# Expert weights of a top-2 mixture loaded as 256-column pairs, eight transfers an expert in place of twelve

## What is computed

```python
gate = ...                                   # (T, 16), two non-zero entries a token
y = jnp.zeros_like(t)
for e in range(16):
    h = jax.nn.silu(t @ w1[e]) * (t @ w3[e])  # w1, w3: 1024 x 512
    y = y + gate[:, e:e + 1] * (h @ w2[e])    # w2: 512 x 1024
x = layer_norm(ALPHA * x + y, ln2_g, ln2_b)
```

## Time and profile before

| | us |
|---|---|
| median of 3 runs | 1128.33 (1127.29 to 1129.90) |
| the profiled execution's own time | 1126.51 |
| its span, first to last instruction | 1125.0 |
| TensorE busy (PE) | 970.7, 86% of the span |
| weight loads into TensorE (PEld) | 832.3, 74% |
| VectorE (DVE) | 705.9, 63% |
| ScalarE (ACT) | 531.7, 47% |
| GpSimd (POOL) | 186.9, 17% |
| SP's queue: 180736 packets, 139.54 MB | 42.9% of 16 DMA engines |

### The profile page before, as it was taken

The page is one execution under the profiler, slowest core; times in us unless marked ns, Lnnn a source line. Parts: engine busy times, 40 slices in busy tenths (PEclk is TensorE's granted clock), DMA queues, the critical chain, the costliest instruction groups (busy, mean ns, idle before and its releaser), DMA issues.

```text
span 1125.0 us, 17021 instructions
## 1 busy us (share of the span) xinstructions
PE 970.7 (86%) x6074; PEld 832.3 (74%) x6074; DVE 705.9 (63%) x1061; ACT 531.7 (47%) x901; POOL 186.9 (17%) x227
## 2 busy tenths in 40 slices
PE   4998999989999999899936959999999999999200
PEld 3777998967777776788836849999999999988100
DVE  3101724555556647665568648888888888885397
ACT  4112512234655546411125647667667667664232
POOL 2000000000000000000004333222332222210474
PEclk8999999989999999999956979999999999999755
DMA  9011020001010011782119999989998999965542
GB/s 241 8 55 38 20 75 20 1 20 38 19 38 20 20 38 38 211 265 91 57 38 213 132 314 304 293 281 290 287 300 277 286 282 292 278 209 204 206 180 94
DMA packets 195058, 170.87 MB, mean 152 GB/s; under 512 B 20400, under 2 KB 172976, under 8 KB 195008
## 3 DMA queue, kind: packets, MB, share of 16 engines
q1 hardware_dynamic: 180736, 139.54, 42.9%
q0 software_dynamic: 11232, 29.47, 7.4%
q10 hardware_dynamic: 3040, 1.19, 0.5%
HBM read 151.21 MB, written 18.95 MB: 151 GB/s over the span
## 4 chain that ended last, share of the span: by engine, by line
PE 76%; DVE 9%; issue 4%; ACT 4%; DMA 3%; POOL 2%; SPq 1%; POOLq 0%; DVEq 0%; ACTq 0%
PE pz L925 15%; PE bank L632 11%; PE bank L634 11%; PE bank L633 11%; PE pz L927 6%; PE pz L784 2%; PE pz L952 2%; PE pz L950 2%; PE bank L797 2%; PE bank L811 2%; PE bank L908 2%; SPq L434 1%; POOL slot_tokens L549 1%; DMA slot_tokens<-tok,rows_u 1%; PE pz L634 1%
## 5 line engine op out<-in xcount | busy, mean ns | idle before, releaser
L925 PE MATMUL pz<-xT,eh 128*128 128x320 f32 x1024 | 266.4, 347 | 2.2 <-DVE gu L1549 1.3
L1536 DVE TENSOR_TENSOR el<-er,eh 128x1024 fp32r<-128x1024 f32 x192 | 229.7, 1220 | 35.7 <-ACT eh L1187 33.5
L927 PE MATMUL pz<-xT,el 128*128 128x160 f32 x1024 | 242.4, 237 | 0.0
L1187 ACT ACTIVATE eh<-er 128x1024 fp32r<-128x1024 f32 x192 | 196.2, 1050 | 7.5 <-DMA er<-in_w_dram 6.8
L927 PEld LDWEIGHTS pz<-xT,el 128*128 128x128 f32 x1024 | 197.1, 192 | 0.6
L925 PEld LDWEIGHTS pz<-xT,eh 128*128 128x128 f32 x1024 | 193.4, 189 | 4.6 <-DVE el L1536 1.5
L1388 DVE TENSOR_TENSOR_SCAN Qs<-Qs 128x128 f32<-128x128 f32 (+7 forms) x48 | 65.0, 1354 | 78.4 <-ACT Qs L1087 78.4
L632 PE MATMUL bank<-xT_hi,w_hi 128*128 128x512 f32 x256 | 105.1, 410 | 10.2 <-DVE w_lo L1265 10.2
L634 PE MATMUL bank<-xT_hi,w_lo 128*128 128x512 f32 x256 | 101.0, 394 | 0.0
L633 PE MATMUL bank<-xT_lo,w_hi 128*128 128x512 f32 x256 | 100.6, 393 | 0.0
L526 POOL MEMSET zidl<- 128x140 uint32 x1 | 0.2, 214 | 444.7 <-ACT aT L1098 444.7
(11 more groups left out here) (261 smaller groups left out, 1847.9 us busy)
## 6 DMA issues: line engine op xcount, KB each, us to landing
er<-in_w_dram SPq DMA_DIRECT2D x192, 512.0 KB, 6.0
w_raw<-in_w_in_dram SPq DMA_DIRECT2D x21, 512.0 KB, 3.8
y_scratch<-yA POOLq DMA_DIRECT2D x16, 512.0 KB, 4.5
x_row<-in_x_dram SPq DMA_DIRECT2D x8, 512.0 KB, 8.3
xres<-in_x_dram SPq DMA_DIRECT2D x8, 512.0 KB, 4.8
x_scratch<-x SPq DMA_DIRECT2D x8, 512.0 KB, 2.9
cx<-x_scratch SPq DMA_DIRECT2D x8, 512.0 KB, 7.7
out_dram<-cx SPq DMA_DIRECT2D x8, 512.0 KB, 2.6
```

Source lines behind the costliest of these rows:

```text
L925: pe.matmul(bank, eh[:, p, ks], xT2[:, k, :, :].rearrange("p a t -> p (a t)"), start=(k == 0), stop=False, skip_group_check=True)
L927: last = pe.matmul(bank[:, 0:TW], el[:, p, ks], xT2[:, k, 0, :], start=False, stop=(k == NK - 1), skip_group_check=True)
L1187: act.activation(eh[:, p, :], er[:, p, :], ACT.Copy).then_inc(S["eh_ok"], 1)
L1536: dve.tensor_tensor(el[:, p, :], er[:, p, :], eh[:, p, :].bitcast(F32), ALU.subtract).then_inc(S["el_ok"], 1)
```

## The change

The w1 and w3 halves of an expert are loaded two column slices at a time. Transfer q (0 to 3) brings 256 columns of w1 (even q) or w3 (odd q): pieces 0 and 2, 1 and 3, 4 and 6, 5 and 7, each 1 MB with runs of 256 floats (1 KB). Transfers 4 to 7 are the w2 pieces as before. In `er` the two slots of a pair hold 8 rows of 256 columns, so that ACT and DVE read a piece as 8 runs of 128 floats at a stride of 256 (raw_piece, as_raw); `eh` and `el` keep their layout. A pair's load waits until DVE is done with the later of the two pieces it overwrites (2, 3, 6, 7).

```diff
--- before.py
+++ after.py
@@ -324,7 +324,7 @@
-        names += [f"e_in{p}" for p in range(NPIECE)]
+        names += [f"e_in{q}" for q in range(2 * NF)]
         names += [f"{n}{i}" for n in ("cg_in",) for i in range(NT)]
         S = {n: sem(n) for n in names}
 
@@ -352,6 +352,16 @@
 
         w_k = I["w_in"][0].rearrange("(k p) n -> p k n", p=P)
 
+        def raw_piece(p):
+
+            if p >= 2 * NF:
+                return er[:, p, :]
+            c0 = (p % 4 // 2) * P
+            return er[:, 4 * (p // 4) + 2 * (p % 2):4 * (p // 4) + 2 * (p % 2) + 2, :].rearrange("p a (k f) -> p (a k) f", f=2 * P)[:, :, c0:c0 + P]
+
+        def as_raw(t, p):
+            return t if p >= 2 * NF else t.rearrange("p (k f) -> p k f", k=NK)
+
         w1v = I["w1"][0].rearrange("e (k p) f -> p e k f", p=P)
         w3v = I["w3"][0].rearrange("e (k p) f -> p e k f", p=P)
         w2v = I["w2"][0].rearrange("e (f p) d -> p e f d", p=P)
@@ -359,16 +369,17 @@
         def load_expert(sp, j, e, first=False):
 
             b = NE * j + e
-            for p in range(NPIECE):
+            for q in range(NF + NF):
                 if not first:
-                    sp.wait_ge(S["el_ok"], NPIECE * b - NPIECE + p + 1)
-                if p < 2 * NF:
-                    src = (w1v, w3v)[p % 2][:, bass.ds(e, 1), :, (p // 2) * P:(p // 2 + 1) * P]
-                    dst = er[:, p:p + 1, :].rearrange("p e (k f) -> p e k f", k=NK)
+                    last = 4 * (q // 2) + 2 + q % 2 if q < NF else NF + q
+                    sp.wait_ge(S["el_ok"], NPIECE * b - NPIECE + last + 1)
+                if q < NF:
+                    src = (w1v, w3v)[q % 2][:, bass.ds(e, 1), :, (q // 2) * 2 * P:(q // 2 + 1) * 2 * P]
+                    dst = er[:, 2 * q:2 * q + 2, :].rearrange("p a (k f) -> p (a k) f", f=2 * P).unsqueeze(1)
                 else:
-                    src = w2v[:, bass.ds(e, 1), p - 2 * NF, :]
-                    dst = er[:, p:p + 1, :]
-                sp.dma_start(dst, src).then_inc(S[f"e_in{p}"], 16)
+                    src = w2v[:, bass.ds(e, 1), q - NF, :]
+                    dst = er[:, NF + q:NF + q + 1, :]
+                sp.dma_start(dst, src).then_inc(S[f"e_in{q}"], 16)
 
         def passes_of(eng, one_pass):
 
@@ -1181,10 +1192,10 @@
 
 
             def piece_hi(b, p):
-                act.wait_ge(S[f"e_in{p}"], 16 * b + 16)
+                act.wait_ge(S[f"e_in{2 * (p // 4) + p % 2 if p < 2 * NF else p - NF}"], 16 * b + 16)
                 if not (isinstance(b, int) and b == 0):
                     act.wait_ge(S["piece_done"], NPIECE * b - NPIECE + p + 1)
-                act.activation(eh[:, p, :], er[:, p, :], ACT.Copy).then_inc(S["eh_ok"], 1)
+                act.activation(as_raw(eh[:, p, :], p), raw_piece(p), ACT.Copy).then_inc(S["eh_ok"], 1)
 
             def x_hi(b, rounds=range(NXR)):
                 for r in rounds:
@@ -1533,7 +1544,7 @@
 
             def piece_lo(b, p):
                 dve.wait_ge(S["eh_ok"], NPIECE * b + p + 1)
-                dve.tensor_tensor(el[:, p, :], er[:, p, :], eh[:, p, :].bitcast(F32), ALU.subtract).then_inc(S["el_ok"], 1)
+                dve.tensor_tensor(as_raw(el[:, p, :], p), raw_piece(p), as_raw(eh[:, p, :].bitcast(F32), p), ALU.subtract).then_inc(S["el_ok"], 1)
 
             def x_lo(b, rounds=range(NXR)):
                 for r in rounds:
```

## The result

The changed kernel takes 1130.70 us, the median of 20 runs (1127.68 to 1133.43), against 1128.23 for the kernel before (20 runs beside it, 1126.22 to 1130.60): ratio 1.0021, 95% interval 1.0013 to 1.0030. It is slower by 0.21%, some 2.4 us, just past what a measurement can tell from nothing. The forecast was 1127.4 and no change.

What follows compares the result with a forecast made beforehand. TensorE bounds the expert stage, except in one dip set by three DMA waits. Terms: 0 steady, 0 strides, 0.9 us less in the dip, giving 1125.6 for the profiled execution and 1127.4 for the median; range 1118.6 to 1133.3.

Steps and rivals of the forecast that it cites:

- The dip: TensorE's 11.96 us stop near 650 us behind scatter, list read and gather; 0.9 us less was forecast there.
- the 11.96: TensorE's stop in us for the gather of expert 2's rows, taken to cover ACT's 4.71 us wait.
- The third rival: In the dip: a pair comes too late for ACT, past some 8 us of cover; slower by 1 or 2 us; chance 0.03.
- The second rival: Scatters of the slot list: longer weight packets ahead of them, slower by 3.3 us, 1131.6; chance 0.22.
- The first rival: In the dip: all three DMA waits scale with a weight byte's time, 3.7 us faster, 1124.6; chance 0.37.
- The sum's 0 for the scatter: In the dip: weight bytes don't fill the engines, so fewer, longer packets shouldn't shorten the scatter: 0.
- 0 in the steady part: From 700 to 1000 us TensorE hides the loads, so faster transfers and later release change nothing.
- 0 for the strides: ACT's and DVE's strided reads of w1 and w3 pieces cost the same as contiguous ones, within one percent.
- 0 for expert 0's load: At 468 us, ahead of later xres loads: 2.1 us shorter, no TensorE time hangs on it, cost 0.
- 65,536 packets fewer: SP's queue in the profile after would have this many packets fewer than its 180,736.
- the estimate: Loads of w1 and w3: 1 KB packets run near 340 GB/s, 2.1 us less an expert, 14% less time a byte.
- the sum's 0.9 us less for the gather: In the dip: the gather's 6.20 us wait scales with the 14% less time a weight byte, 0.9 us less.

Runs made afterwards that it cites:

- the gather gone: Expert 2's rows fetched behind the scatters with expert 1's row numbers, without waiting for the slot list: kernel before 1118.29 us (0.9924), changed kernel 1123.36 us (0.9971).
- the late release alone: Kernel before with its twelve 512-byte-run transfers, but the pairs' release and order (0, 2, 1, 3): 1129.68 us, ratio 1.0016.
- strides: Changed layout and strided reads, but twelve 512 KB transfers with 512-byte runs, each released by its own piece: 1128.28 us, ratio 1.0002.
- experts 1 and 2 by pieces: Changed kernel, but experts 1 and 2 loaded in twelve early-released pieces with 512-byte runs, the others as pairs: 1128.36 us, ratio 1.0003.
- the hold: SP issues no load of expert 2 until all scatters have landed: kernel before 1122.81 us (0.9964), changed kernel 1119.19 us (0.9935).

## Why the prediction was wrong

**The step that failed** is in "The dip": "ACT waits 4.71 us for piece 1 of expert 2 in the dip; that is covered by the 11.96." The wait was read off the kernel before and covered as it stood. That the change itself lengthens it was worked out only for the steady part, where a released buffer has 17.7 us until it is read. In the dip the same release has no such room: DVE frees piece 2 of expert 1 about 4.4 us after piece 0, transfer 0 then takes 29.2 us from issue to landing, and ACT can't begin before all of it is in. ACT's wait for piece 0 went from none to 5.96 and 9.14 us in two profiles, and TensorE's cover from 11.96 to 3.00 and 3.19.

**The third rival** named this mechanism and its place, with a chance of 0.03 and 1 or 2 us. It expected the pair 7 us later and let it be 8 us late before anything costs; where the 8 come from it doesn't say. The lateness was well put: piece 1 was copied at 650.86 and 652.79 against 642.95, which is 6.7 and 7.7 us later once the 1.2 and 2.1 us are taken off by which expert 0's last transposes already begin later (601.67, 602.89 and 603.77). What it left out is the clock. TensorE's first products of expert 1 end 9.8 and 10.4 us later by the same count, because behind the new stop they run at half clock for some 6 us, which takes 2.5 to 3 us of the cover. That its 1 or 2 us stand near the measured 2.4 is luck in part, since its threshold wasn't passed.

**What stays open** is the last link. The profiles of the changed kernel show the gather last, and yet the time rose by 2.4 us; with the gather gone it costs 5.1 us. A cover of 3 us makes it likely that in some executions the weights come last, and the clock behind the stop was worth 1.0 us in one profile; but no profile shows the weights last, and the kernel with the late release alone had a cover of 9.7 us. A rival that these runs don't exclude is that the later loads lengthen the DMA waits in the dip. The profiles don't favour it: from the issue of the last scatter to TensorE's resumption it takes 34.4 and 34.1 us in the changed kernel, 34.3 with the late release, but also 34.4 and 33.8 in two kernels without a loss (strides, experts 1 and 2 by pieces), and 32.5 in the one profile of the kernel before.

**The second rival**, longer packets ahead of the scatters, isn't the cause: the last scatter took 15.71 and 15.37 us with 1 KB packets, and 14.80, 15.13, 15.06 and 13.92 with 512-byte packets, on average 0.8 us less and not 3.3; and the loss came without longer packets too. The turn-taking rule of the Trainium skill ("DMA: Bandwidth & Descriptors", "Queues, rings and completion order") would have made this rival's 3.3 us the time to expect; these runs don't show them.

**The first rival** was right that the engines are shared, and wrong that the waits scale with the time of a weight byte: that fell and the waits didn't. The sum's 0 for the scatter was right in that it got no shorter, but what held it up was left unsaid: the hold shows that the weights do.

**The steps that held**: 0 in the steady part, 0 for the strides, 0 for expert 0's load (these within the 0.1 to 0.2% that the runs can tell), 65,536 packets fewer. The transfer time gained more than the estimate (364 GB/s against 338), and none of it reached the path. The 512 bytes that the Trainium skill gives as enough for line rate ("DMA: Bandwidth & Descriptors", "Specifications") aren't borne out here, 290 against 364 GB/s.

**A term that failed beside them** is the sum's 0.9 us less for the gather, scaled with the 14%. It took 6.68 and 6.42 us, against 6.20.

## What to carry to other kernels

Joining transfers joins their releases: a buffer pair is free when its later half is, and ready when its last byte is in. Price that at the place with the least lead (here the start of a pipeline with small transfers in the same queues), not in the steady state, and price a cover with the changed wait inside it, the clock behind a new stop included. A step that a stop hides is best measured by taking the stop away, as the 2.4 us here became 5.1.

## What the runs showed of the hardware

Sixteen scatters of 4-byte elements with a weight stream in the same engines wait far longer than their bytes would suggest: the last one landed after 13.9 to 15.7 us with the weights of the next expert beside it, and after 4.1 to 7.3 without. The weights moved only 0.60 MB in 8 us beside them; no run leaves the scatters out, so that they slow the weights isn't shown. And the granted clock stayed at 1.2 GHz for a while after TensorE resumed: 3.8 us behind a stop of 12 us, 6.3 and 3.0 us behind stops of 3.4 and 3.0 in the first profile of the changed kernel, 5.8 us behind one of 3.2 in the second.
